# Perceptron entry of a two-layer block: VectorE's order of halves, modulation, splits and tile 1's scaling

## What is computed

```python
    mixed = merged @ w_o
    x = layer_norm(ALPHA * x + g1 * mixed) * ln1_g + ln1_b

    u2 = layer_norm(x) * (1 + sc2) + sh2
    hdn = jnp.square(jax.nn.relu(u2 @ w_up + b_up))
    x = layer_norm(ALPHA * x + g2 * (hdn @ w_down)) * ln2_g + ln2_b
```

## Time and profile before

| | |
|---|---|
| median of 3 runs | 1325.86 us (1323.12 to 1327.38) |
| profiled execution | 1327.98 us |
| its span | 1326.2 us |
| TensorE | 1284.2 us busy, 97% of the span |
| VectorE | 931.5 us, 70% |
| ScalarE | 522.5 us, 39% |
| GpSimd | 108.0 us, 8% |
| mean granted clock of TensorE | 0.99 |

### The profile page before, as it was taken

How to read it: one execution, slowest core, us unless ns; L and a number is a source line. 1 busy time by engine, 2 the same in 40 slices (tenths; PEclk the granted TensorE clock), 3 DMA queues, 4 the chain that set the end, 5 groups by cost and what they waited for, 6 DMA issues and landing times.

```text
span 1326.2 us, 18821 instructions
## 1 busy us (share of the span) xinstructions
PE 1284.2 (97%) x7785; PEld 1062.7 (80%) x7785; DVE 931.5 (70%) x1223; ACT 522.5 (39%) x805; POOL 108.0 (8%) x152
## 2 busy tenths in 40 slices
PE   5999999999999999999999999999999999999996
PEld 2798756547965569989988898976998998899895
DVE  4867677658759655877898666675587789654557
ACT  3322246214357143553344434333344434443432
POOL 2200110100000110011002000001011100000000
PEclk9999999999989999999999999999999999999998
DMA  9643550316620584687974776537567795355551
GB/s 373 226 145 113 177 190 1 126 65 225 205 95 1 193 272 157 242 278 267 322 264 141 242 263 235 191 127 254 174 238 272 269 335 173 123 185 185 185 187 57
DMA packets 104910, 257.75 MB, mean 194 GB/s; under 512 B 8213, under 2 KB 11766, under 8 KB 104570
## 3 DMA queue, kind: packets, MB, share of 16 engines
q1 hardware_dynamic: 80872, 172.40, 38.6%
q0 software_dynamic: 20192, 75.58, 15.9%
q10 hardware_dynamic: 3762, 8.57, 1.8%
HBM read 255.49 MB, written 1.05 MB: 193 GB/s over the span
## 4 chain that ended last, share of the span: by engine, by line
PE 85%; DVE 7%; ACT 3%; DMA 2%; issue 2%; POOL 1%; POOLq 0%; ACTq 0%; DVEq 0%
PE bank L823 81%; PE bank L990 4%; DVE weights_low L2351 2%; DMA start_ring<-in_w_mod_dram 1%; DMA weight_ring<-in_w_in_dram 1%; ACT weights_high L1736 1%; ACT even_A L1870 1%; DVE even_A L2303 1%; DVE statistics L2318 0%; DVE x L2317 0%; DVE xn L2311 0%; DVE modulation_sums L2206 0%; DVE negated_maxima L2298 0%; DVE forget_of_keys L2788 0%; POOL inverse_roots L721 0%
## 5 line engine op out<-in xcount | busy, mean ns | idle before, releaser
L2351 DVE TENSOR_TENSOR weights_low<-weight_ring,weights_high 128x2048 fp32r<-128x2048 f32 (+1 forms) x120 | 261.7, 2184 | 205.3 <-ACT weights_high L1736 205.0
L1736 ACT ACTIVATE weights_high<-weight_ring 128x2048 fp32r<-128x2048 f32 (+1 forms) x120 | 219.7, 1831 | 319.3 <-PE bank L823 294.5
L823 PE MATMUL bank<-uT_high,weights_high 128*128 128x256 f32 (+1 forms) x1136 | 324.0, 285 | 0.1
L823 PE MATMUL bank<-uT_high,weights_low 128*128 128x256 f32 (+1 forms) x1136 | 321.3, 283 | 0.0
L823 PE MATMUL bank<-uT_low,weights_high 128*128 128x256 f32 (+1 forms) x1136 | 321.3, 283 | 0.0
L823 PEld LDWEIGHTS bank<-uT_high,weights_high 128*128 128x128 f32 (+1 forms) x1136 | 216.1, 190 | 2.8 <-issue 1.0
L823 PEld LDWEIGHTS bank<-uT_low,weights_high 128*128 128x128 f32 (+1 forms) x1136 | 216.2, 190 | 1.2
L823 PEld LDWEIGHTS bank<-uT_high,weights_low 128*128 128x128 f32 (+1 forms) x1136 | 216.2, 190 | 0.5
L2206 DVE SCALAR_TENSOR_TENSOR modulation_sums<-modulation_ring,silu_c_columns,modulation_sums 128x1024 f32<-128x1024 f32 x112 | 143.7, 1283 | 10.1 <-DMA modulation_ring<-in_w_mod_dram 5.5
L823 PE MATMUL bank<-weights_high,hidden_high 128*128 128x512 f32 x256 | 100.2, 391 | 0.2 <-DVE weights_low L2351 0.2
L823 PE MATMUL bank<-weights_low,hidden_high 128*128 128x512 f32 x256 | 99.8, 390 | 0.0
(11 more groups left out here) (337 smaller groups left out, 2205.7 us busy)
## 6 DMA issues: line engine op xcount, KB each, us to landing
weight_ring<-in_w_in_dram SPq DMA_DIRECT2D x52, 1024.0 KB, 6.2
modulation_ring<-in_w_ada_dram POOLq DMA_DIRECT2D x48, 1024.0 KB, 6.5
weight_ring<-in_w_down_dram SPq DMA_DIRECT2D x32, 1024.0 KB, 4.9
weight_ring<-in_w_up_dram SPq DMA_DIRECT2D x28, 1024.0 KB, 5.3
modulation_ring<-in_w_mod_dram POOLq DMA_DIRECT2D x16, 1024.0 KB, 5.6
weight_ring<-in_o_w_in_dram SPq DMA_DIRECT2D x10, 1024.0 KB, 5.1
norm_rows<-in_w_branch_dram SPq DMA_DIRECT2D x16, 512.0 KB, 5.7
weight_ring<-in_w_o_dram SPq DMA_DIRECT2D x8, 1024.0 KB, 7.9
```

The costliest lines, as they stand in the source:

```text
L823: return track(pe.matmul(*args, **kw))
L1736: act.activation(ring[:, s, c0:kn * cols], wring[:, slot, c0:kn * cols], ACT.Copy).then_inc(S["high_ready"], 1)
L2351: dve.tensor_tensor(lo[:, s, c0:kn * cols], wring[:, slot, c0:kn * cols], hi[:, s, c0:kn * cols].bitcast(F32), ALU.subtract).then_inc(w_fr ...
```

## The change

Five edits, all in the stage above but for one:

- VectorE does both halves of tile 0, its variance, centring and scaling before it touches tile 1 (before: half 0 of tile 1 came first).
- `centred` is two instructions of 512 columns in place of one of 1024; no wait stands between them. This holds for all eight uses in the kernel.
- ScalarE modulates both blocks of tile 0; VectorE did the second before.
- VectorE's order behind tile 1's variance is now: modulation columns, centring of tile 1, split of tile 0's block 0, scaling of tile 1, split of block 1, late low part.
- TensorE does the second row sum behind tile 0's transposes, and one of the stand-in products goes.

```diff
@@ TensorE @@
                     done(ins, ("mod", 1))
                     signal(ins, S["acc_used"])
-                    keep_busy(idle, 1)
                     o = start(("mod", 2))
                     columns_of_sums(2, o, range(4))
                     keep_busy(idle, 1)
                     ins = columns_of_sums(2, o, range(4, KD))
                     done(ins, ("mod", 2))
                     signal(ins, S["acc_used"])
+                    turn_tile(0, "x2T", TC)
                     signal(row(1), S["acc_used"])
 
                 sums_of_second()
-                turn_tile(0, "x2T", TC)
                 keep_busy(start(("up", 0, 0)), 3)
@@ ScalarE @@
-                modulate_block("x2T", 0, 0, mcol2)
+                for b in range(2):
+                    modulate_block("x2T", 0, b, mcol2)
                 squares_of_tile(sec, 2, 1)
@@ VectorE, centred(i) @@
-                    link(dve.scalar_tensor_tensor(out=x[:, i, :], in0=x[:, i, :], scalar=mv[:, i, 0:1],
-                                                  in1=lnrow[:, 0, :], op0=ALU.subtract, op1=ALU.mult))
+                    for h in range(2):
+                        cols = slice(COLS * h, COLS * h + COLS)
+                        ins = dve.scalar_tensor_tensor(out=x[:, i, cols], in0=x[:, i, cols], scalar=mv[:, i, 0:1],
+                                                       in1=lnrow[:, 0, cols], op0=ALU.subtract, op1=ALU.mult)
+                    link(ins)
@@ VectorE, residual_of_mixed(m) @@
-                    link(halves_of_tile("o", 1, 0))
                     link(halves_of_tile("o", 0, 1))
                     variance(0, False, LN_EPS)
                     centred(0)
                     scaled(0, m, total[:, 0:1]).then_inc(S["affine"], 1)
+                    link(halves_of_tile("o", 1, 0))
                     link(halves_of_tile("o", 1, 1))
                     variance(1, False, LN_EPS)
-                    centred(1)
                     mod_columns(1, mcol2, 0)
                     mod_columns(2, mcol2, 1)
+                    centred(1)
+                    split_block("x2T", 0, 0)
                     scaled(1, m + 2, total[:, 1:2]).then_inc(S["affine"], 1)
+                    split_block("x2T", 0, 1)
+                    low_late(1, WCOLS // 2, WCOLS // 2)
                     for c in (1, 2):
                         copied(("mod", c))
-                    modulate_block("x2T", 0, 1, mcol2)
-                    for b in range(2):
-                        split_block("x2T", 0, b)
-                    low_late(1, WCOLS // 2, WCOLS // 2)
                     modulate_block("x2T", 1, 0, mcol2)
```

## The result

| | before | the change |
|---|---|---|
| median, us | 1322.43 (1318.3 to 1327.38, 14 runs) | 1329.32 (1326.48 to 1335.84, 14 runs) |
| ratio, 95% interval | 1 | 1.0054 (1.0039 to 1.0069) |
| profiled execution, its span | 1327.98, 1326.2 | 1328.75, 1326.9 |
| mean granted clock | 0.99 | 0.99 |

The account below looks back on a forecast made before the run. TensorE's entry into the perceptron was taken to bound each layer. 2 x (2.1 delayed scaling + 0.4 clock) - 0.45 centring = +4.55 us on the profiled 1327.98, less 2.1 for the median: 1330.5 us, range 1327.0 to 1334.5.

Parts of the forecast that it names:

- the hold: VectorE, tile 1's scaling queued behind tile 0's first split, which waits for ScalarE's modulation: tile 1's transposes +2.1 us a layer.
- the clock: TensorE around tile 0's transposes: granted clock falls to half in both layers, +0.4 us a layer, between 0 and 1.9.
- the case of the forecast: Half clock at tile 0's transposes in both layers, slower work behind them fitting into 2.8 us of idle; chance 0.46.
- Tile 0's halves first: VectorE, tile 0's scaling 2.2 us sooner, but ScalarE's up1 weights let only 0.4 us reach the squares, at 695.8.
- That ScalarE now modulates both blocks hides in this: ScalarE modulates until 703.6, before tile 1's squares can start at 704.5, so its second block adds nothing.
- Its signs: VectorE idle 1.5 to 2 us before tile 0's first split; TensorE 2 to 3 us before tile 1's transposes, 9.3 behind tile 0's.
- The rival that it reaches the dense products: Half clock also slows the up products behind tile 1's transposes, 1.5 us a layer: +7.6 us, 1333.5 us; chance 0.12.
- a thinner row with idle in it: TensorE before tile 0's transposes: only one stand-in and 1.6 us of idle left, the reason given for losing full clock.
- The halved centring: GpSimd's root gets through between VectorE's two 512-column centring pieces: -0.45 us, once, at the kernel's last scaling.
- Cost VectorE 0.03 us more: VectorE's centring as two 512-column pieces takes 1.30 us against 1.27 for one of 1024 columns.
- The sum: Whole kernel: 2 x (2.1 + 0.4) - 0.45 = +4.55 us, giving 1330.5 us.

Follow-up runs that it names:

- The second profile of the change: The unaltered change profiled once more against the kernel before; stages 31.59 and 31.60 us (28.28 before), one run, no ratio.
- The run with the late bank: Against the change, TensorE waits for the second row sum's PSUM bank only at that row sum; ratio to the kernel before 1.0046, stages 30.70 and 30.73 us.
- the profile with both edits back: Against the change, tile 1's scaling again ahead of tile 0's splits and TensorE's old order restored; stages 34.10 and 30.17 us, ratio to the kernel before 1.0056.
- the scaling first: Against the change, tile 1's scaling again ahead of both splits of tile 0; stages 31.08 and 30.62 us, ratio to the kernel before 1.0032.
- the second reordered version: Against the first reordering, VectorE centres tile 1 before the modulation columns and modulates tile 0's block 1 itself; ratio to the kernel before 0.9981.
- the kernel with TensorE's order alone: Against the kernel before, one stand-in less and the second row sum behind tile 0's transposes; stages 29.49 and 29.78 us, ratio 1.0019.
- the two reordered kernels: Against the change: tile 0's squares before up1's second weights, scaling before splits, late bank, both stand-ins; ratios to the kernel before 0.9988 and 0.9981.

## Why the prediction was right

Forecast +4.6 us by the hold and the clock; measured +7.1 (5.2 to 9.1). The mechanism and its rows were right, one term was missing. That the time itself came so close (1330.5 forecast, 1329.32 measured) is in part luck: the forecast started from the median of three runs, 1325.86 us, which was 3.4 us above that of fourteen, and the missing 2.5 us lay the other way.

The second profile of the change (clock at half once a layer, the case of the forecast), layer 1, whose stage starts at 1114.82:

```profile
1126.19 0.19 ACT L2002 ACTIVATE second_norm<-second_norm 128x1 f32<-128x1 f32 x1
...
1130.22 1.97 PE L990 MATMUL bank<-constants,xn 128*128 128x128 f32 x8 [1.30 <-ACT xn L2011]
...
1133.06 0.43 DVE L2688 CAST uT_high<-mergedT 128x512 fp32r<-128x512 f32 x1 [2.62 <-ACT mergedT L2026]
...
1139.95 1.10 PE L990 MATMUL bank<-constants,xn 128*128 128x128 f32 x8 [1.09 <-ACT xn L2011]
```

Beside the prediction's steps, in us of the stage:

| step | forecast | measured |
|---|---|---|
| tile 0's squares | 10.6 | 11.4 |
| tile 0's transposes | 14.6 | 15.4 |
| VectorE's first split (with 0.4 for the clock) | 17.3 | 18.2 |
| tile 1's transposes (with 0.4) | 24.3 | 25.1 |

- **Tile 0's halves first: wrong.** "The squares can start at 695.8 at best" took the start of ScalarE's weights as set by the end of the output products, "which the change doesn't touch". It is set by the product behind them, and the change puts that one behind a wait for a bank. This 0.8 us is nearly all that separates the two columns above. The run with the late bank took it away and landed on 10.5 and 24.27.
- **The hold: right in place and size.** 2.39 us by itself, forecast 2.1. But it isn't worth 2.1 when it is taken out of the change, only 1.0 (31.13 against 30.17). "That ScalarE now modulates both blocks hides in this" was true, and is the reason: with the hold gone, those 1.5 us come out. In the profile with both edits back, layer 1, tile 1's squares start at 1133.30, without idle behind ScalarE's eight modulations (1130.55, 2.90 us). So with the scaling first, the change's tile 1 transposes are still 2.3 us later than before (24.18 against 21.84).
- **Its signs.** VectorE idled 2.61 us in front of the split (1.5 to 2 forecast), and tile 1's transposes stood 9.7 us behind tile 0's (1139.95 - 1130.22; 9.3 forecast). TensorE's wait for xn in front of them was only 0.9 to 1.6 us in three of the four layers (2 to 3 forecast), since its work at half clock filled the rest.
- **The clock: right.** It fell in all four layers of the change (and in 10 of 10 with its order on TensorE); eight transposes took 1.97 us, and the chain lost about 0.4. The row sum and the stand-ins at half rate hid in the new idle. The rival that it reaches the dense products came true in one layer of four of the change. But the reason given, a thinner row with idle in it, isn't shown: the last section has a fall ahead of the idle, and the order of before lost the clock in 5 of 14 layers.
- **The halved centring: right in kind.** GpSimd gets in between the halves: 1.0 us for 1.5. The last scaling starts 1.51 us behind the variance (1322.63 - 1321.12) in place of 1.86: 0.35 gained, forecast 0.45. "Cost VectorE 0.03 us more" was wrong: the pair takes 1.41 us, since a half lasts 0.74 (0.69 was assumed) and the second starts 0.66 behind the first (0.61 was assumed). It also gains 0.4 us a layer at tile 0, which I had left out because ScalarE's weights seemed to stand in front; in the kernel before they end at 695.8, and the squares started at 696.20.
- **The sum:** forecast 2 x 2.5 - 0.45; by the profiles 2 x 3.3 - 0.35 = 6.3 us, inside the measured interval. The 0.8 us a layer of the bank are the term that was missing.

## What to carry to other kernels

In front of every instruction that one moves on an in-order engine, ask what is queued behind it: a split that waits for another engine costs nothing for itself, but holds the scaling behind it, on which the next tile's whole chain hangs. A wait taken early for a resource needed late (the bank) can hold signals that ride on the instruction behind it, so look up on which instruction a signal really rides. Edits that share an idle time don't add up: alone the hold costs 2.4, ScalarE's second block 1.5 and the order of the halves 1.7 us a layer, all of the change together 3.3.

## What the runs showed of the hardware

- GpSimd waits for the VectorE instruction that runs, not for the one queued behind it. A root that started inside a centring of 1.27 us took 1.51 to 1.54 us; inside the first of two halves of 0.74 us each it took 0.98 to 1.00. In both forms it ended 0.40 us behind the end of the instruction in which it had started (1320.07 + 1.27 and 1320.23 + 1.51 before; 1321.19 + 0.74 and 1321.35 + 0.98 in the change). The rule of the Trainium skill (SBUF — State Buffer, on the shared port pair: the one that starts first has it for the whole instruction) agrees as far as GpSimd's wait goes. That the waiting root then holds VectorE's next instruction isn't seen: the second half ran beside the rest of the root, and all sixteen halves of the change's profile lasted 0.74 to 0.75 us.
- A write of GpSimd does hold a cast of VectorE: a cast that started inside a memset of GpSimd (698.50, 0.95 us) took 0.95 us in place of 0.43, in the second reordered version. The kernel before has the same pair at 468.90 (memset) and 469.19 us (cast, 0.94).

```profile
698.50 0.95 POOL L683 MEMSET modulation_sums<- 128x1024 f32 x1
...
696.31 0.43 DVE L2691 CAST uT_high<-mergedT 128x512 fp32r<-128x512 f32 x1 [0.42 <-ACT mergedT L2029]
...
698.78 0.95 DVE L2691 CAST uT_high<-mergedT 128x512 fp32r<-128x512 f32 x1
```

- A busy TensorE can lose its clock. In the kernel with TensorE's order alone the granted clock was 0.99 from 694 to 696 us, where one-column products ran without a gap, and 0.50 from 696 to 698, though TensorE was still busy until 696.76, where the idle time of 1.50 us before tile 0's transposes begins. With one more stand-in and the row sum there it fell in 5 of 14 layers; in the two reordered kernels, with the stand-in but the row sum behind the transposes, in 1 of 4. What decides between the two outcomes, no run here shows.
